# A mixture-of-experts block as two halves of 32 tokens in four column groups, with the 128x128 turns on TensorE replaced by 32x32 turns on VectorE

## The reference, cut to what matters

```python
expert = best[:, None] * EXPERTS_PER_GROUP + local      # two of 16 experts for each token
...
xb = jnp.zeros((n_blocks * MOE_BLOCK, dm), x.dtype).at[dest].set(x[tok])
...
def expert_block(args):
    xe, e = args
    return (jax.nn.silu(xe @ w_gate[e]) * (xe @ w_up[e])) @ w_down[e]
...
y_slot = yb[dest] * wts.reshape(-1)[order][:, None].astype(x.dtype)
return jax.ops.segment_sum(y_slot, tok, num_segments=n_tok)
```

## Time and profile before

| | |
|---|---|
| median of 3 runs | 1444.61 us (1433.77 to 1446.91) |
| profiled execution, its own time | 1438.59 us |
| its span, first to last instruction | 1436.8 us |
| TensorE (matmul) busy | 1337.9 us, 93% |
| VectorE, ScalarE, GpSimd busy | 414.1, 263.3, 235.1 us |
| mean granted clock of TensorE | 0.969 |
| read from HBM, written | 286.18 MB, 33.10 MB |
| chain that ended last | PE 72%, DMA 13%, DVE 5%, issue 3%, SyncE's queue 3% |

### The profile page before, as it was taken

One profiled execution on the slowest core, in us unless ns is written; L12 is line 12 of the kernel. 1 busy time (PEld: TensorE's weight loads), 2 busy tenths in 40 slices (PEclk: granted clock), 3 DMA queues, 4 the chain that ended last, 5 costly groups with the idle time before them and its releaser, 6 DMA issues.

```text
span 1436.8 us, 25808 instructions
## 1 busy us (share of the span) xinstructions
PE 1337.9 (93%) x10155; PEld 837.8 (58%) x10156; DVE 414.1 (29%) x886; ACT 263.3 (18%) x401; POOL 235.1 (16%) x285
## 2 busy tenths in 40 slices
PE   5899999977999999999958999999999999999975
PEld 3688778756676677764434455555555555454532
DVE  4692870375622210113362000000000000000065
ACT  3305002243125000001111111111111111111102
POOL 0033403200000000000023022012022222223310
PEclk9899999998999999999979999999999999999997
DMA  7459632345430412514088619819949999999993
GB/s 303 150 130 391 149 71 68 80 148 194 148 131 3 177 44 78 215 39 167 15 336 343 257 44 383 340 29 350 393 151 398 379 403 381 404 379 397 383 401 122
DMA packets 92365, 322.30 MB, mean 224 GB/s; under 512 B 12000, under 2 KB 12384, under 8 KB 91536
## 3 DMA queue, kind: packets, MB, share of 16 engines
q1 hardware_dynamic: 72304, 268.77, 49.5%
q0 software_dynamic: 11216, 38.41, 8.7%
q10 hardware_dynamic: 8784, 14.24, 3.2%
HBM read 286.18 MB, written 33.10 MB: 222 GB/s over the span
## 4 chain that ended last, share of the span: by engine, by line
PE 72%; DMA 13%; DVE 5%; issue 3%; SPq 3%; ACT 2%; POOL 0%; POOLq 0%; DVEq 0%; ACTq 0%
PE ps L2236 18%; PE ps L1771 11%; PE ps L2247 10%; PE ps L1759 9%; DMA expert_w<-in_w_down 9%; PE ps L2150 5%; PE ps L2199 5%; SPq L557 3%; PE ps L1863 2%; PE ps L1946 2%; DMA expert_w<-in_w_up 2%; PE ps L2242 1%; DMA x_sorted<-h,router_ints 1%; PE ps L1832 1%; PE ps L2226 1%
## 5 line engine op out<-in xcount | busy, mean ns | idle before, releaser
L2236 PE MATMUL ps<-expert_w,x_block_t 128*64 128x256 f32 x3584 | 403.8, 382 | 15.1 <-issue 6.5
L2236 PEld LDWEIGHTS ps<-expert_w,x_block_t 128*64 128x64 f32 x3584 | 256.0, 137 | 163.1 <-issue 31.5
L2247 PE MATMUL ps<-expert_w,act_t 128*64 128x512 f32 x896 | 213.9, 604 | 3.6 <-DMA expert_w<-in_w_down 2.6
L1771 PE MATMUL ps<-h_t,weight_ring 128*128 128x320 f32 x640 | 178.4, 435 | 0.0
L1771 PEld LDWEIGHTS ps<-h_t,weight_ring 128*128 128x128 f32 x640 | 121.5, 191 | 50.9 <-issue 2.8
L1759 PE MATMUL ps<-h_t,weight_ring 128*128 128x320 f32 x512 | 145.4, 447 | 2.8 <-ACT h_t L749 2.8
L1669 DVE TENSOR_TENSOR activations<-silu_tmp,ps 128x256 f32<-128x256 f32 x56 | 23.6, 421 | 375.9 <-ACT silu_tmp L967 375.9
L1759 PEld LDWEIGHTS ps<-h_t,weight_ring 128*128 128x128 f32 x512 | 100.1, 197 | 45.2 <-issue 6.9
L2247 PEld LDWEIGHTS ps<-expert_w,act_t 128*64 128x64 f32 x896 | 57.8, 136 | 103.1 <-issue 78.2
L692 POOL COPY expert_w<-staged 128x1024 f32<-128x1024 f32 x42 | 43.9, 1044 | 414.5 <-PE ps L2236 269.0
L1690 DVE COPY y_block<-ps 128x512 f32<-128x512 f32 x25 | 17.3, 692 | 188.7 <-PE ps L2247 188.7
(11 more groups left out here) (362 smaller groups left out, 1224.2 us busy)
## 6 DMA issues: line engine op xcount, KB each, us to landing
expert_w<-in_w_down SPq DMA_DIRECT2D x128, 512.0 KB, 13.2
weight_ring<-in_stream SPq DMA_DIRECT2D x98, 512.0 KB, 4.9
expert_w<-in_w_gate SPq DMA_DIRECT2D x58, 512.0 KB, 11.8
expert_w<-in_w_up SPq DMA_DIRECT2D x58, 512.0 KB, 12.8
staged<-in_w_gate SPq DMA_DIRECT2D x28, 512.0 KB, 14.0
gathered<-in_w_gate SPq DMA_DIRECT2D x28, 512.0 KB, 16.0
gathered<-in_w_up SPq DMA_DIRECT2D x28, 512.0 KB, 16.5
x_sorted<-zero POOLq DMA_DIRECT2D x18, 512.0 KB, 13.8
```

Source lines behind the costliest of these rows:

```text
L1771: last = mm(pair(job)[:, a, :], w[:, k, :], h_t[:, k, a * HALF:(a + 1) * HALF], start=(k == 0), stop=(k == KD - 1))
L2236: last = mm(ps[MB * g:MB * g + MB, 2 * half + w, 0:256], x_blk_t[:, 2 * kp + k2, :], rows[:, at_col:at_col + 256], start=(kp == 0 and k2 = ...
L2247: last = mm(ps[MB * half:MB * half + MB, 4, :], act_t[:, 4 * (f // 4) + 2 * (f % 2) + f // 2 % 2, :], w_slot[3 * f + 2][:, 4 * half:4 * ha ...
```

## The change

**Tokens.** A block is two halves h of SUB = 32 tokens. The array works as four column groups of 32: `gates(h, k)` takes 128 input rows and 32 tokens, and each of the four groups g multiplies them with 256 gate columns and 256 up columns, 512 in one matmul. Half 0 goes through all eight k, then half 1 goes through them again. `down(h, j)` is the same with 256 columns a group. The sum of columns times groups is what it was: 64 matmuls of 512 columns in four groups for `gates` (before 64 of 256 in two), 64 of 256 in four for `down` (before 16 of 512 in two).

**Turns.** `turn_x`, `turn_act` and the four PSUM copies of ScalarE are gone; VectorE turns 32x32 blocks, 128x512 for the tokens and 128x256 for each half of the products. For that the weights' input rows are permuted on the host, and rows are moved between `x_sorted`, `y_sorted` and SBUF in pieces of 1 KB instead of 2 KB.

**Releases.** `gu_done` now rises in half 1 only, and `down_done` too. The first half has one semaphore for its end, `half_done`.

**The last two blocks** are taken out of the loop and written out; TensorE's loop now ends with `last2`. They use `down_both`, which is the old form of `down`, and the turn of `last_tokens` stands between the gates and the down part of block 26.

```diff
+SUB = MB // 2
+Q = 4
+QC = D // Q
...
-            def copy_x():
-                nc.scalar.activation(x_blk_t[:, :, :].rearrange("p (g j) t -> p g j t", g=2),
-                                     ps[:, 6, :].rearrange("p (j g t) -> p g j t", j=4, g=2), ACT.Copy).then_inc(xt_copied, 1)
...
-                    for a in range(2):
-                        act.wait_ge(gu_done, i * KF + (4 * a + 4))
-                        take_gates(a)
-                        act.wait_ge(act_turned, i * 2 + (a + 1))
-                        copy_act(a)
-                    act.wait_ge(xt_done, i + 2)
-                    copy_x()
+                    act.wait_ge(half_done, i + 1)
+                    take_gates(0)
+                    act.wait_ge(gu_done, i * KF + KF)
+                    take_gates(1)
+                    act.wait_ge(xt_copied, i + 2)
                     load_x(i * MB + 2 * MB)
...
+            def turn_act(h):
+                vec.transpose(act_t[:, :, h, :], acts[:, h, :].rearrange("p (j l) -> p j l", l=SUB)).then_inc(act_ready, 1)
+
+            def turn_x():
+                vec.transpose(x_blk_t[:, :, :, :].rearrange("p h k t -> p (h k t)"),
+                              x_blk[:, :, :].rearrange("p h c -> p (h c)")).then_inc(xt_copied, 1)
...
+                    for h in range(2):
+                        dve.wait_ge(silu_ready, i * 2 + (h + 1))
+                        take_prod(h)
+                        dve.wait_ge(prod_ready, i * 2 + (h + 1))
+                        turn_act(h)
+                    dve.wait_ge(x_blk_in, i * 32 + 32)
+                    turn_x()
...
+            def gates(h, k):
+                for g in range(Q):
+                    last = mm(ps[SUB * g:SUB * g + SUB, h, :].rearrange("p (w c) -> p w c", w=2), x_blk_t[:, h, k, :],
+                              w_pair[k][:, :, QC * g:QC * g + QC], start=(k == 0), stop=(k == KD - 1))
+                if h == 1:
+                    last.then_inc(gu_done, 1)
+                elif k == KD - 1:
+                    last.then_inc(half_done, 1)
+
+            def down(h, j):
+                for g in range(Q):
+                    last = mm(ps[SUB * g:SUB * g + SUB, 4, QC * h:QC * h + QC], act_t[:, j, h, :],
+                              w_down_sb[j][:, QC * g:QC * g + QC],
+                              start=(j == 0), stop=(j == KF - 1))
+                if h == 1:
+                    last.then_inc(down_done, 1)
...
+                    pe.wait_ge(xt_copied, i + 1)
+                    for k in range(KD):
+                        wait_gates(e, k)
+                        gates(0, k)
+                    for k in range(KD):
+                        gates(1, k)
+                    pe.wait_ge(act_ready, i * 2 + 1)
+                    pe.wait_ge(y_copied, i + 1)
+                    for j in range(KF):
+                        pe.wait_ge(dn_in[j], e * 16 + 16)
+                        down(0, j)
+                    pe.wait_ge(act_ready, i * 2 + 2)
+                    for j in range(KF):
+                        down(1, j)
```

More of the change, by code:

```diff
@@ L248, in hybrid_step @@
                  y_last_rows[:, 0:D], y_last_rows[:, D:2 * D], at("staged5", qs0 + 36864, [P, D])[:, :]] + got
[L249 removed]
+        assert end + 9216 <= top[0] and len(stage) == STAGED and qs0 + 40960 <= end - 23 * 4096
         fin = [at(f"final{i}", pool0 + (10 + i) * 4096, [P, D]) for i in range(CH)]
@@ L1701, in _ @@
                 add_some(ahead)
-                dve.wait_ge(silu_ready, last2 * 2 + (2 * u + 1))
-                take_prod(0)
-                add_some(beside)
-                dve.wait_ge(silu_ready, last2 * 2 + (2 * u + 2))
-                take_prod(1)
+                for h in range(2):
+                    dve.wait_ge(silu_ready, last2 * 2 + (2 * u + h + 1))
+                    take_prod(h)
+                    dve.wait_ge(prod_ready, last2 * 2 + (2 * u + h + 1))
+                    turn_act(h)
+                    if h == 0:
+                        add_some(beside)
+                if u == 0:
+                    dve.wait_ge(x_blk_in, last2 * 32 + 32)
+                    turn_x()
                 add_some(behind)
@@ L2223, in _ @@
             pe.wait_ge(pick0_ready, 1)
-            def turn_x():
-                for j in range(4):
-                    last = nc.tensor.transpose(ps[:, 6, j * P:(j + 1) * P], x_blk[:, j * P:(j + 1) * P], ident)
-                last.then_inc(xt_done, 1)
-            def gates(s):
-                half, kp = s // 4, s % 4
-                for k2 in range(2):
-                    for w in range(2):
-                        rows = w_slot[3 * s + w][:, :, :].rearrange("p k c -> p (k c)")
-                        for g in range(2):
-                            at_col = 512 * k2 + 256 * g
-                            last = mm(ps[MB * g:MB * g + MB, 2 * half + w, 0:256], x_blk_t[:, 2 * kp + k2, :],
-                                      rows[:, at_col:at_col + 256], start=(kp == 0 and k2 == 0), stop=(kp == 3 and k2 == 1))
-                last.then_inc(gu_done, 1)
@@ L2240, in turn_act @@
-            def turn_act(a):
-                for j in range(2):
-                    last = nc.tensor.transpose(ps[:, 5 + 2 * a, j * P:(j + 1) * P], acts[:, a, j * P:(j + 1) * P], ident)
-                last.then_inc(act_turned, 1)
-            def down(f):
+            def gates(h, k):
[6 more added lines that the diff above has]
+                    last.then_inc(half_done, 1)
@@ L2280, in _ @@
-            pe.wait_ge(route_ready, 1)
-            blocks = pe.value_load(rint[0:1, TOTAL:TOTAL + 1], min_val=EXPERTS, max_val=NBLK)
+            for k in range(KD):
+                pe.wait_ge(gu_in[k], 32)
+                gates(0, k)
+            for k in range(KD):
+                gates(1, k)
+            for h in range(2):
+                pe.wait_ge(act_ready, h + 1)
+                for j in range(KF):
+                    if h == 0:
+                        pe.wait_ge(dn_in[j], 16)
+                    down(h, j)
```

232 lines of the change are left out of this document (102 added, 130 removed).

## The result

The changed kernel takes **1536.01 us** (median of 4 runs, 1531.73 to 1541.11), the kernel before 1443.09 us beside it (1433.77 to 1446.91). The ratio is **1.0655** (95% interval 1.0594 to 1.0717): 93 us slower, where 30 were predicted.

The account below looks back on a forecast made before the run. TensorE is 99% busy, but DMA is also full where one- and two-block experts alternate, so weights are waited for. +29 + 3.6 - 5 + 4.4 - 10 + 8 = +30 us on 1438.59: 1468, forecast 1455 to 1482 (65%).

Parts of the forecast that it names:

- pieces of 1 KB: Twice as many packets for x and y: taken as 0, with 2 us a triple of blocks kept for the range.
- Free block: A block that waits for nothing: 13.8 gates + 0.2 switch + 7.1 down + 0.4 loop = 21.5 us, 1.0 less.
- Triple: Last block of an expert (A), next expert's single block (B), following expert's first (C): 73.6 us for 68.65; six, +29 us.
- Five free blocks: Blocks 2, 3, 7, 8 and 12, waiting for nothing and in no triple: -1.0 us each, -5 us.
- Block 1: It waits for its tokens and last gate tile, and ends at 806.0 us instead of 802.4: +3.6 us.
- The loop's end: Eight empty iterations of TensorE's loop, 0.75 us each, now ahead of block 26: 6.0 us.
- The tail: From block 25 on: +4.4 us up to block 27's last down matmul, -10 us behind it.
- The clock: TensorE's lower clock after waiting, in six triples' third blocks and blocks 1 and 27: 1.0 us each, +8, range 0 to 17.
- (1): Rival: TensorE is the bound everywhere, blocks lose 1.0 us each and the tail 10: 1401 us; 9%.
- (2): Rival: waiting real but cheaper; clock up, loop's end hidden, down at 6.9, release shift absorbed; triple +3.3, 1447 us; 15%.
- (3): Rival: loop code no longer fits what TensorE holds, 24 jumps back wait 1 to 1.5 us for fetches: 1485 us; 7%.
- (4): Rival: something else, such as four groups of 512 columns not running side by side, tens of us a block; 4%.

Follow-up runs that it names:

- e10_before_1k: The kernel before with its y stores in 1 KB pieces, as four DMAs a block with 64 tokens as slowest dimension: 1438.93 us, ratio 1.0011.
- e1_spread: The changed kernel with x loads and y stores issued as four DMAs a block, one per column quarter, 32 tokens as slowest dimension: 1463.6 us, ratio 1.0151.
- e9_pairs: e1_spread plus half 1 of gate tiles 0-4 before half 0 of 5-7, and five staged loads of each pair's second expert before the first's remaining 14: 1430.33 us.

## Why the prediction was wrong

**The step that failed** is the one on pieces of 1 KB, "I take 0 ... and keep 2 us a triple for the range". It asked what a packet costs and how many there are, and not which engines carry them. The measured term is 11.8 us a triple, six of them 71 us: 9.2 of landings that come later by the four loaded engines, and 2.6 of the lower clock behind the longer waits. The forecast's 1468 lacks those 71 us; put back, they give 1539 where the profiled execution took 1531.7. The changed kernel's source showed the cause: the outermost dimension of the new pattern is `q`, of size 4. The other uncertainty in that step, packets by count, is nil for y's stores (e10_before_1k).

With that one term taken out, e1_spread is the kernel that I had predicted, 1463.6 us for 1468. That it comes so close is in part luck, since errors of both signs cancel. Its terms, from the two profiled spans, 1462.1 - 1436.8 = 25.3 us:

- **Free block**: 21.5 predicted, 20.95 measured: 13.94 gates, 6.91 down, 0.1 between iterations. Gates 13.8 and the hidden VectorE chain (a turn of 0.45 us, in the cover of 3.5) were right. Four groups cost nothing extra: 128 down records of 256 columns in 6.91 us are 54 ns each, half of the 108 ns that the same columns take in two groups. The trace doesn't show the 60 cycles a matmul that the Trainium skill ("TensorEngine Tiling (Array Packing)", Instruction Overhead) gives; the choice for the row was right. The 0.4 for the loop's end is 0.1: too high.
- **Triple**: 73.6 predicted without the clock's share, 73.2 measured; +4.6 each, 27.7 us for +29. The last gate tile landed at 58.2 us (911.49 - 853.27), where I had 58.1. This step held in mechanism and size.
- **Five free blocks**: -5 predicted, -7.6 measured, by the 0.5 us above.
- **Block 1**: blocks 0 and 1 together take 64.2 us and took 58.0, +6.2 where the sum has +3.6 and 1.0 of the clock; 2.2 of the 6.2 are the lower clock (10.08 us for the last 72 gate records, in place of 7.9). In three other kernels with x and y spread they take 61.1 to 62.5. Too low by up to 1.6 us.
- **The loop's end**: the empty iterations ahead of block 26 show as 6.40 us of "issue" (6.0 predicted). The count and the price were both off: 9 iterations run empty here and 7 before, not 8 and 6, and each takes 0.74 us in the trace.
- **The tail**: from block 27's last down product to the end of the span 20.6 us (some 20 predicted; of its sum 2.81 + 0.8 make 3.6, not 3.4, which changes nothing). From the start of block 27 on 55.6 us, before 63.6: -8.0. Of it -9.3 lie behind the last down product, for -10, and +1.3 ahead of it. The prediction's +4.4 - 10 = -5.6 is for everything from block 25 on, since it let the wait for expert 15's tiles use up block 25's gain; so measured it is +4.7 (block 25 and the loop's end) - 0.5 (block 26) - 8.0 = -3.8.
- **The clock**: +8 predicted, about 6 measured, but not where it was put. The six C's lose nothing: their products behind the last tile take 7.93 us for 72 records, 7.84 at the full rate, and the mean of 0.84 in C's window is the lower level falling in the waiting. Blocks 1 and 27 lose 2.2 and 2.0 us on the same records (10.08 and 9.88 us), and block 26, which wasn't named, 1.6 (15.53 us of gates for 13.94). These us stand in the terms above already. In the changed kernel, whose waits are longer, all six C's lose, 10.1 to 10.9 us for those 72 records, the 2.6 us a triple named above, 16 of the 71.

The terms then are 2.8 us of difference ahead of the blocks (well inside the scatter of that part) + 6.2 + 27.7 - 7.6 - 3.8 = 25.3.

**The rivals.** (1) TensorE the bound everywhere, 1401: refuted, C waits; even e9_pairs, which removes most of the wait, is at 1430. (2) Waiting cheaper, 1447: refuted at 85 us a triple; for the mechanism apart from the four engines, 73.2 against its 71.95, it is refuted too, though three of its four conditions held in the triples of e1_spread (clock up, loop's end hidden, down at 6.9); the shift of the releases wasn't absorbed. (3) Instruction fetches in the loop, 1485: refuted; between 801 and 1340 us the changed kernel has one packet of instructions, as the earlier trace rows. No run shows what a fetch would cost, so its 1 to 1.5 us stay an assumption, and the loop body before has 336 matmul and weight-load instructions, 168 of each by the earlier trace rows, not 352:

```profile
q10 hardware_dynamic: 10695, 10.62, 5.9%
q14 instruction: 1, 0.01, 0.0%
```

(4) had 4% for something else, and something else it was. The signs named for being right, C blocks standing for tiles, a DMA share below 0.97 (0.95 in C), PEclk below 1, came true and would not have told the missed cause; triples of 73 to 75 us were the sign that failed.

## What to carry to other kernels

When a rearranged load or store puts a small dimension outermost, count the DMA engines that it will use, whatever its bytes: in this kernel the bulk loads beside it landed when their most loaded engine was done. Issue the same pieces as more DMAs with the long dimension outermost, and check by the number of small packets and by slices in which the DMA share rests at 4/16. Where a stretch is full of transfers, an edit that shortens the work behind one landing or starts one transfer early is worth only what the last landing moves, so count the tiles in front of it.

## What the runs showed of the hardware

- Skew adds up: 0.5 MB a block on 4 engines, 5.9 us of packets on each, left the last four counts of a tile's landing 10 us behind the twelfth within a triple (78.6 and 68.8 us), and the twelve engines that were idle at the end did not take over.
- The count of small packets gives the engines: 1760, 424, 3392, 1032, 1936 and 2592 over a constant 10240 in six kernels, each to one as DMAs x engines.
- A store of 256 KB on two engines takes 28 us to land beside full weight traffic, where the packets alone are 128 x 46 ns = 5.9 us on each. That it queues behind the weights' packets on those engines fits this, but was not read packet by packet.
- A VectorE turn of 32x32 blocks takes 0.45 us for 128x256 and 0.67 us for 128x512 elements of float32.
- An empty guarded iteration of the loop takes TensorE's sequencer 0.74 us (7 of them before, 9 after).
